# A two-layer hybrid transformer trunk on one core: where gathered rows and the router's input are transposed

## The reference, cut to what matters

```python
for l in range(DEPTH):                                  # DEPTH = 2
    h = _rmsnorm(x, mix_norm[l])
    ...                                                 # ya, yb, yc: the three mixers
    x = x + jnp.concatenate([ya, yb, yc], axis=-1) @ w_out[l]
    x = x + _expert_choice_ffn(_rmsnorm(x, ffn_norm[l]), router[l], w_gate[l], w_up[l], w_down[l])

def _expert_choice_ffn(x, router, w_gate, w_up, w_down):
    xf = x.reshape(T, D)
    aff = jax.nn.softmax((xf @ router).astype(jnp.float32), axis=-1)
    gate, idx = lax.top_k(aff.T, cap)                   # cap = 128 (sample) and 32 (prompt) per expert
    xs = xf[idx]
    hid = jax.nn.silu(jnp.einsum('ecd,edf->ecf', xs, w_gate)) * jnp.einsum('ecd,edf->ecf', xs, w_up)
    ye = jnp.einsum('ecf,efd->ecd', hid, w_down) * gate[..., None].astype(x.dtype)
    return jnp.zeros((T, D), x.dtype).at[idx.reshape(-1)].add(ye.reshape(-1, D)).reshape(B, S, D)
```

## Time and profile before

| | before |
|---|---|
| median of 3 runs (lowest, highest) | 2354.94 us (2353.14, 2355.67) |
| the profiled execution: its time, its span | 2355.69 us, 2354.1 us |
| PE busy | 2303.9 us (98%) |
| DVE busy | 995.4 us (42%) |
| ACT, POOL busy | 622.3 us (26%), 538.7 us (23%) |
| mean granted TensorE clock | 0.995 |
| DMA | 352.18 MB, mean 150 GB/s |

### The profile page before, as it was taken

The page is one execution under the profiler, slowest core; times in us unless marked ns, Lnnn a source line. Parts: engine busy times, 40 slices in busy tenths (PEclk is TensorE's granted clock), DMA queues, the critical chain, the costliest instruction groups (busy, mean ns, idle before and its releaser), DMA issues.

```text
span 2354.1 us, 33210 instructions
## 1 busy us (share of the span) xinstructions
PE 2303.9 (98%) x13054; PEld 1644.7 (70%) x13054; DVE 995.4 (42%) x1855; ACT 622.3 (26%) x1445; POOL 538.7 (23%) x550
## 2 busy tenths in 40 slices
PE   8999999999999999999999999999999999999998
PEld 6556587874556888877775665878655568887786
DVE  3654476586554111111136535756864631111111
ACT  3221333553342111111132312335533411111111
POOL 1003453243211111111110034632432111111111
PEclk9999999999999999999999999999999999999999
DMA  4011131221228988778430112312112389878883
GB/s 152 21 37 55 54 131 63 81 81 63 74 96 302 321 280 275 264 266 286 122 124 21 36 54 74 105 54 90 72 73 81 117 290 317 280 255 279 279 284 73
DMA packets 149364, 352.18 MB, mean 150 GB/s; under 512 B 9909, under 2 KB 38073, under 8 KB 149210
## 3 DMA queue, kind: packets, MB, share of 16 engines
q1 hardware_dynamic: 134234, 308.11, 36.6%
q0 software_dynamic: 14976, 41.95, 7.2%
HBM read 307.75 MB, written 42.28 MB: 149 GB/s over the span
## 4 chain that ended last, share of the span: by engine, by line
PE 93%; DVE 2%; DMA 1%; ACT 1%; issue 1%; POOL 0%; SPq 0%; DVEq 0%; ACTq 0%; POOLq 0%
PE ps L1813 88%; PE ps L2349 1%; PE ps L2098 1%; PE ps L2159 1%; PE ps L1832 1%; DVE TMP L1237 1%; DMA HT<-h_sample,idxs 0%; PE ps L1865 0%; DMA y_sample<-SCR,idxs 0%; PE ps L2110 0%; DVE TMP L1246 0%; PE ps L2339 0%; ACT SCR L1042 0%; DVE SCR L1237 0%; POOL SCR L759 0%
## 5 line engine op out<-in xcount | busy, mean ns | idle before, releaser
L1813 PE MATMUL ps<-MID,HT 128*128 128x512 f32 (+3 forms) x2560 | 693.2, 490 | 4.7 <-DMA MID<-w_in 3.8
L1813 PEld LDWEIGHTS ps<-HT,MID 128*128 128x128 f32 x4096 | 557.6, 191 | 16.1 <-issue 15.1
L1813 PE MATMUL ps<-HT,MID 128*128 128x160 f32 (+1 forms) x4096 | 565.6, 299 | 0.6 <-DVE HT L1237 0.4
L1813 PEld LDWEIGHTS ps<-MID,HT 128*128 128x128 f32 (+1 forms) x2560 | 292.6, 157 | 245.8 <-issue 207.2
L1813 PE MATMUL ps<-RING,HT 128*128 128x256 f32 (+2 forms) x1760 | 395.8, 392 | 1.7 <-DVE RING L1241 1.3
L1813 PEld LDWEIGHTS ps<-RING,HT 128*128 128x128 f32 (+1 forms) x1760 | 310.7, 189 | 83.5 <-issue 40.7
L1813 PE MATMUL ps<-HT,RING 128*128 128x512 f32 (+1 forms) x960 | 350.0, 522 | 0.0
L1246 DVE SCALAR_TENSOR_TENSOR HT<-HT,ps 128x160 f32<-128x160 f32 (+1 forms) x128 | 40.9, 319 | 683.1 <-ACT HT L1201 658.5
L1813 PEld LDWEIGHTS ps<-HT,RING 128*128 128x128 f32 x960 | 180.2, 190 | 157.8 <-issue 149.8
L849 POOL DMA_INDIRECT y_prompt<-SCR,idxp x32 | 50.5, 1578 | 618.4 <-ACT SCR L1211 617.8
L1201 ACT ACTIVATE HT<-ps 128x160 f32<-128x160 f32 (+1 forms) x128 | 38.6, 302 | 519.8 <-PE ps L1813 511.5
(11 more groups left out here) (264 smaller groups left out, 2159.3 us busy)
## 6 DMA issues: line engine op xcount, KB each, us to landing
MID<-w_gate SPq DMA_DIRECT2D x32, 2048.0 KB
MID<-w_up SPq DMA_DIRECT2D x32, 2048.0 KB
MID<-w_down SPq DMA_DIRECT2D x32, 2048.0 KB, 15.3
RING<-w_in SPq DMA_DIRECT2D x20, 1024.0 KB, 5.3
SCR<-cs_rows SPq DMA_DIRECT2D x20, 1024.0 KB, 5.1
MID<-w_out SPq DMA_DIRECT2D x8, 1024.0 KB, 6.6
y_sample<-RING SPq DMA_DIRECT2D x16, 512.0 KB, 2.7
h_sample<-HT SPq DMA_DIRECT2D x16, 512.0 KB, 2.6
```

Source lines behind the costliest of these rows:

```text
L1813: return pe.matmul(out, a, b, start=start, stop=stop)
```

## The change: what it does

In short:

- **Router input.** For chunks 0 to 6 of the attention stage PE's `turn_h2` and DVE's `keep_h2` go. DVE transposes `XO` itself: `turn_h2(c, a0, a1)` issues, for each group `a` of 32 rows, four transposes of 32 partitions by 256 elements (eight 32x32 blocks each), 16 for a chunk. Group 0 stands where `keep_h2(n-1, 0)` stood, group 1 behind `keep_y(n+1, 0)`, groups 2 and 3 behind `take_x(n)`. `logits` keeps its place on PE and its wait for `h2t_copied`, and from chunk 1 to 6 waits for `lg_shift` too. SP's reload of `XO` waits for DVE's transposes.
- **Gathered rows.** From expert 1 on the tokens, and from quad 1 on the prompt rows, are transposed by DVE straight from the gather buffer into `XT`: 8 transposes behind slice 1, 8 behind slice 2, for experts 4 and up 4 more for the prompt rows behind slice 3. Then two multiplications in place by the norm's weight (`weigh_tokens`). PE keeps the transposes of expert 0's tokens and of quad 0.
- **Last expert.** PE makes the prompt part first, then the two halves; ACT scales in that order; POOL scatters the sample rows in two halves of 512 columns, with row indices 2i and 2i+1 made by two small DVE operations (`idxh`).

The core of the diff (waits that are only renumbered are left out):

```diff
                         if c + 2 < NC:
                             sp.wait_ge(x_stored[c % 2], 16 * (c // 2 + 1))
-                            sp.wait_ge(h2t_made, 2 * c + 2)
+                            if c < LAST_SAMPLE:
+                                sp.wait_ge(h2t_copied, 2 * c + 2)
+                            else:
+                                sp.wait_ge(h2t_made, 2)
...
                     def gather(e):
                         if e >= 3:
-                            pool.wait_ge(g_turned, turn_at(e - 3, 1) + 1)
+                            if e == 3:
+                                pool.wait_ge(g_turned, 2)
+                            else:
+                                pool.wait_ge(xt_made, e - 3)
...
+                        if e == E - 1:
+                            pool.wait_ge(scattered_s, seen["halves"] + 16 * e)
+                            for hf in range(2):
+                                pool.wait_ge(down_scaled, 3 * e + 2 + hf)
+                                pool.indirect_dma_start(ys2, bass.IndirectOffsetOnAxis(ap=idxh[:, hf:hf + 1], axis=0),
+                                                        YO[e % 2][:, hf * 512:(hf + 1) * 512], None,
+                                                        compute_op=ALU.add, bounds_check=2 * SEQS[1] - 1).then_inc(scattered_s, 16)
+                            break
...
+                    def turn_h2(c, a0, a1):
+
+                        if a0 == 0 and c >= 1:
+                            dve.wait_ge(parts_made, c)
+                        for a in range(a0, a1):
+                            for b in range(4):
+                                turned = link(dve.transpose(H2T[32 * b:32 * b + 32, :, 32 * a:32 * a + 32],
+                                                            XO[c % 2][32 * a:32 * a + 32, :].rearrange("p (k b i) -> p k b i", b=4, i=32)[:, :, b, :]),
+                                              h2t_copied if b == 3 and a % 2 == 1 else dve_chain, wait=False)
...
                             attn_shift(n + 2, 0)
-                        keep_h2(n - 1, 0)
+                        turn_h2(n - 1, 0, 1)
                         keep_y(n + 1, 0)
+                        turn_h2(n - 1, 1, 2)
                         if n + 2 < NC:
                             attn_shift(n + 2, 1)
                         take_x(n)
-                        keep_h2(n - 1, 1)
+                        turn_h2(n - 1, 2, 4)
                         keep_y(n + 1, 1)
...
+                    for hf in range(2):
+                        ts(idxh[:, hf:hf + 1], idxs[:, E - 1:E], 2.0, float(hf), ALU.mult, ALU.add)
...
+                    def turn_rows(e, at, rows):
+
+                        for b in range(4):
+                            turned = link(dve.transpose(XT[e % 2][32 * b:32 * b + 32, :, at:at + 32],
+                                                        rows.rearrange("p (k b i) -> p k b i", b=4, i=32)[:, :, b, :]), wait=False)
+                        return turned
...
+                    def weigh_tokens(e, turned, cols):
+
+                        dve.wait_ge(dve_chain, turned)
+                        for j in range(2):
+                            v = XT[e % 2][:, 4 * j:4 * j + 4, 0:cols]
+                            tt(v, v, wide(pr("gffn")[:, 4 * j:4 * j + 4], cols), ALU.mult, xt_made if j == 1 else dve_chain)
...
-                            if f == KF - 3 and e + 1 < E:
-                                if (e + 1) % QUAD == 0:
-                                    for j in range(2):
-                                        copy_quad((e + 1) // QUAD, j)
-                                spread_quad(e + 1)
-                            if f == KF - 2 and e + 1 < E:
-                                copy_tokens(e + 1, 0)
+                            if e + 1 < E and 1 <= f <= 2:
+                                turned = turn_tokens(e + 1, 2 * f - 2, 2 * f)
...
-                        if e + 1 < E:
-                            copy_tokens(e + 1, 1)
+                        if e + 1 < QUAD:
+                            spread_quad(e + 1)
+                            weigh_tokens(e + 1, turned, CAPS)
+                        elif e + 1 < E:
+                            weigh_tokens(e + 1, turn_prompt(e + 1), TOK)
...
                         pe.wait_ge(h2t_copied, 2 * c + 2)
+                        if 1 <= c < LAST_SAMPLE:
+                            pe.wait_ge(lg_shift, c)
...
-                        turn_h2(n - 1, 0)
                         out_proj(n, 0, 5, 6)
...
                         out_proj(n, 0, 7, 8)
-                        turn_h2(n - 1, 1)
                         out_proj(n, 1, 0, 1)
...
                         if e >= 1:
-                            pe.wait_ge(g_copied, copied(turn_at(e, 1) + 1))
-                            pe.wait_ge(quad_spread, e + 2)
+                            pe.wait_ge(xt_made, e)
...
-                        else:
+                        elif e < E - 1:
                             down_half(0)
                             down_prompt()
+                            down_half(1)
+                        else:
+                            down_prompt()
+                            down_half(0)
                             down_half(1)
```

More of the change, by code:

```diff
@@ L162, in program @@
         idxp = sb("idxp", E, U32)
+        idxh = sb("idxh", 2, U32)
         idxus = sb("idxus", CAPS // 4 + CAPP, U32)
@@ L497, in counts @@
         def counts(layer):
-            return {"x": 16 * layer, "scatter": 16 * E * layer,
+            return {"x": 16 * layer, "scatter": 16 * E * layer, "halves": 16 * (E + 1) * layer,
                     "gather": [16 * layer * len(range(j, E, 3)) for j in range(3)],
@@ L567, in _ @@
                     else:
-                        sp.wait_ge(scattered_s, seen["scatter"])
+                        sp.wait_ge(scattered_s, seen["halves"])
                     for c in range(NP, NC):
@@ L676, in _ @@
                         pool.wait_ge(scattered_p, seen["scatter"])
-                        pool.wait_ge(scattered_s, seen["scatter"])
+                        pool.wait_ge(scattered_s, seen["halves"])
                     for r in RAW:
@@ L862, in _ @@
                         pool.wait_ge(scattered_p, seen["scatter"] + 16 * E)
-                        pool.wait_ge(scattered_s, seen["scatter"] + 16 * E)
+                        pool.wait_ge(scattered_s, seen["halves"] + 16 * (E + 1))
                     leave_layer(pool, layer)
@@ L1203, in _ @@
                             act.wait_ge(scattered_p, seen["scatter"] + 16 * (e - 1))
-                            act.wait_ge(scattered_s, seen["scatter"] + 16 * (e - 1))
+                            act.wait_ge(scattered_s, seen["halves"] + 16 * (e - 1))
                         def scale_half(hf):
@@ L1770, in spread_quad, with turn_tokens, turn_prompt @@
                         link(dve.tensor_copy(XT[e % 2][:, k0:k1, CAPS:TOK], XTP[:, k0:k1, CAPP * r:CAPP * (r + 1)]), quad_spread)
+                    def turn_rows(e, at, rows):
[3 more added lines that the diff above has]
+                        return turned
+                    def turn_tokens(e, a0, a1):
+                        if a0 == 0:
+                            dve.wait_ge(gathered[e % 3], seen["gather"][e % 3] + 16 * (e // 3 + 1))
+                        for a in range(a0, a1):
+                            turned = turn_rows(e, 32 * a, XG[e % 3][32 * a:32 * a + 32, :])
+                        return turned
+                    def turn_prompt(e):
+                        q, r = divmod(e, QUAD)
+                        dve.wait_ge(quad_gathered[q % 2], seen["quad"][q % 2] + 16 * (q // 2 + 1))
+                        return turn_rows(e, CAPS, XGP[q % 2][CAPP * r:CAPP * (r + 1), :])
+                    def weigh_tokens(e, turned, cols):
[3 more added lines that the diff above has]
+                            tt(v, v, wide(pr("gffn")[:, 4 * j:4 * j + 4], cols), ALU.mult, xt_made if j == 1 else dve_chain)
                     for e in range(E):
@@ L2406, in _ @@
                             last.then_inc(gu_made, 1)
-                            if f == KF - 3 and (e + 1) % QUAD == 0 and e + 1 < E:
-                                for j in range(2):
-                                    turn_quad((e + 1) // QUAD, j)
-                            if f == KF - 2 and 1 <= e < E - 1:
-                                turn_tokens(e + 1, 0)
                         if e == 0:
                             for j in range(2):
-                                turn_quad(0, j)
-                            turn_tokens(1, 0)
-                        elif e + 1 < E:
-                            turn_tokens(e + 1, 1)
+                                turn_quad(j)
                         pe.wait_ge([ed_loaded0, ed_loaded1][e % 2], 16 * (e // 2 + 1))
@@ L2436, in down_prompt @@
                             for f in range(KF):
+                                if e == E - 1:
```

(1 more changed line is left out.)

78 lines of the change are left out of this document (36 added, 42 removed).

## The result

The kernel after takes 2394.35 us (median of 4 runs, 2392.97 to 2395.47), the kernel before beside it 2355.09 (4 runs, 2353.14 to 2355.67): 1.0166 times as long, 95% interval 1.0154 to 1.0178. The forecast was 2375.5 in a range of 2336 to 2400, and slower. The profiled execution took 2395.1 us, its span is 2393.6, against 2354.1 before. So 39.5 us of span have to be found.

The account below looks back on a forecast made before the run. PE's instruction stream was taken as the bound. Experts and tail -36.6, chunk loop +45.1 and clock +12 gave net +20.5 on 2355.7 us, 2376.2, or 2375.5 as median; range 2336 to 2400.

Parts of the forecast that it names:

- What leaves PE: Removed PE transpose calls: 15.8 us per layer in the experts, about 1 in expert 0, 6.0 in the chunk loop.
- Rival E: Expert stage: PE's slots bring nothing because weight loads become the bound; 2407 us, chance 0.05.
- What a DVE transpose costs: Each 32x256 DVE transpose was put at a spacing of 0.45 us, a group of four at 1.8 us.
- C: DVE's transposes run as fast as its fast copy, spacing 0.20 us; 2321 us, chance 0.12.
- B: DVE's transposes overlap, spacing 0.335 us; 2348 us, chance 0.20.
- D: A DVE transpose costs 0.72 us, so HID is late in 14 experts per layer; 2513 us, chance 0.03.
- The wait on the router's product: Chunk loop: PE waits for DVE before logits in seven rounds, 28.6 us per layer, 22.6 net of saved slots.
- The clock: Chunk loop: the waits lower PE's clock, 1.7 us each; half of 14 falls taken, 12 us.
- the forecast of 24 to 25 us for a round: Sign in the chunk loop: rounds take 24 to 25 us in place of 21.4.
- Experts, DVE: Expert stage: DVE needs 4.3 us against PE's 4.35 per slice; HID of slice 3 keeps 0.9 us cover, cost 0.
- The last expert: Tail: scattering sample rows in two halves saves 1.5 us in each of two layers.
- forecast A: The main forecast: waits on logits outweigh the freed slots; own range 2363 to 2390 us, chance 0.60.

Follow-up runs that it names:

- experiment 2: Kernel before with only the gathered-row transposes moved to DVE; chunk loop, last expert's order and single scatter as before: 2321.85 us, ratio 0.9864.
- experiment 6: Kernel after with each DVE transpose of gathered rows issued as two of 32x128 on the same partitions: 2396.87 us in one run.
- Experiment 4: Kernel after with transpose groups 0 and 1 both ahead of keep_y(n+1, 0) on DVE: 2348.03 us, ratio 0.9978 to the kernel before.
- Experiment 5: Kernel after with six unread products of 384 columns on PE ahead of each router's product in the loop: 2364.97 us, ratio 1.0043 to before.

## Why the prediction was right, and where its size was off

**What leaves PE.** Right. Of PE's 480 transposes of these three kinds 80 are left, and the chain of the expert stage is one piece of PE (start, us, what), where the earlier trace rows shows it cut by calls of 0.44 us:

```profile
849.93 340.38 PE ps L1856 x2284
```

The down products of neighbouring experts start 26.31 us apart:

```profile
869.73 9.09 PE L1856 MATMUL ps<-MID,HT 128*128 128x512 f32 x48
896.04 9.09 PE L1856 MATMUL ps<-MID,HT 128*128 128x512 f32 x48
```

I had said 26.3. The two expert stages lost 34.0 us; 2 x (15.8 + 1) is 33.6, and experiment 2 gives 33.1. Rival E is refuted. One small thing was missing in the sum: before expert 0's first products PE now waits 0.51 us a layer for DVE's copy of the transposed rows, which it did not before.

**What a DVE transpose costs.** The group of the experts' transposes (count | busy, mean ns | idle before), after:

```profile
L1798 DVE STREAM_TRANSPOSE HT<-HT 32x256 f32<-32x256 f32 x576 | 251.0, 436 | 18.4
L1643 DVE STREAM_TRANSPOSE HT<-RING 32x256 f32<-32x256 f32 x224 | 97.6, 436 | 7.2
```

0.436 us against my 0.425 of the earlier trace rows, and four take 1.83, so a spacing of 0.46 to 0.47 against 0.45. C (0.20), B (0.335) and D (0.72) fall. The chain in expert 0 shows them one by one:

```profile
778.00 0.43 DVE HT L1798
778.46 0.43 DVE HT L1798
```

By that spacing the Trainium skill's rule ("VectorE: DVE Perf Modes", "Two Vector instructions with no wait between them") agrees with the trace, and experiment 6 shows both sides of it: 0.24 us apart at 0.30 us long on the same partitions, held until the end on others. The duration of a neighbour of its size (0.425) gave the duration here; whether the output's partitions change decides if the overlap comes off it.

**The wait on the router's product.** Right: 58.2 us in 14 waits against 2 x 28.6 = 57.2. Four a layer were put at 4.3 and are 4.32, the others at 3.75 to 3.95 and are 3.79 to 4.01. Experiment 4 confirms the geometry behind it, one T less for one group moved.

**The clock.** This is the step that failed, in its size. I priced a fall at 1.7 us from one short case and let half of the 14 waits bring one: 12 us. Both halves of that were too low. It fell in each of the 14 rounds, not in half of them, and the falls were dearer than 1.7 us. The loops grew by 79.2 us; less 58.2 of waits and plus 12.0 of freed slots (28 calls of 0.43), 33.0 are left. Experiment 5 gives 29.4 to 31.6 by taking the fall away and nothing else. That is 2.1 to 2.4 us a round where I had 0.85 on average. With it the sum would have come to 2393 to 2397. The rows above say why: from 608 to 620 the grant was 0.71, 0.50 and 0.94, which by my own measure is (0.29 + 0.50 + 0.06) x 4 = 3.4 us, twice the case of the earlier trace rows; only what lay in the wait cost nothing. Ten of the 14 rounds are of this kind. The other four are like the earlier trace rows, as round 7:

```profile
712.00:716.00 4.00, 0.01 (x1) 0.01 (x2) 3.72 (x10) 2.17 (x9) 0.00 (x0) 0.94 0.00 0
716.00:720.00 4.00, 4.00 (x35) 2.77 (x36) 1.16 (x4) 0.27 (x1) 1.89 (x1) 0.64 0.37 131
```

(0.06 + 0.36) x 4 is 1.7. One case with short gaps before it could not tell that a wait of 4 us brings the longer kind.

The same error is in the forecast of 24 to 25 us for a round: the slots and the wait make 21.4 + 4.3 - 0.9 = 24.8, and the clock makes it 27.4.

**Experts, DVE.** Right in that no later expert waits. Slice 3 and what lies behind it are covered by the down product. In expert 14, DVE's second eight transposes, then the two operations of HID of slice 3:

```profile
1156.31 3.71 DVE L1798 STREAM_TRANSPOSE HT<-HT 32x256 f32<-32x256 f32 x8
1160.05 0.32 DVE L1260 SCALAR_TENSOR_TENSOR HT<-HT,ps 128x160 f32<-128x160 f32 x1
1160.40 0.32 DVE L1251 TENSOR_TENSOR HT<-HT,ps 128x160 f32<-128x160 f32 x1
```

The down product of that expert starts at 1159.19 and comes to slice 3 three slices of 0.86 us later, at 1161.77. HID is there at 1160.72, so 1.05 us of cover are left, where I had 0.9. Experiment 6 used them up. PE's waits on DVE's two-operand line that writes this memory (L1251, before L1237) are 2.4 us in the whole kernel against 1.4, and none of them is in the experts' one long piece.

**The last expert.** Mechanism right, size short: 3.1 us in layer 0 and 1.3 in layer 1, 4.4 against 3.0 (4.6 by experiment 2). POOL's issues at the end, after, answering to the earlier trace rows:

```profile
2384.31 1.55 POOL L862 DMA_INDIRECT y_sample<-SCR,idxh  x1 [2.30 <-ACT SCR L1219]
2387.68 1.55 POOL L862 DMA_INDIRECT y_sample<-SCR,idxh  x1 [1.82 <-ACT SCR L1219]
```

The issue of half the bytes takes 1.55 us, as the whole did (1.56): the saving is in what comes behind it, 4.4 us to the end in place of 5.6. Why layer 0 saved more than twice that is open. There the scatter took 8.29 us from issue to landing before and its second half 5.15 after, and the next layer's load of prompt rows, which started with it before (1173.99 and 1174.00), now starts 3.35 us ahead of it; no run separates the two.

**Sum of the steps** (forecast, measured): waits net of slots +45.1, +46.2; clock +12, +33.0; experts and tail -36.6, -38.4. The 21 us missing in the forecast are one term. The result also lies above forecast A's own range, 2363 to 2390, whose upper end priced a fall in every round at 1.7 us. That it lies inside 2336 to 2400 is owed to the margin above 2390, which no term of the sum gave; that much is luck.

## What to carry to other kernels

Moving work from a full engine to one that is nearly idle pays where the receiver has a cover of its own, as here under the down product, and costs the whole delay where the result sits between two steps of the full engine: ask when the other engine delivers, not how busy it is. A wait of some microseconds on TensorE has two prices, its length and the low clock behind it; here waits of 3.8 to 4.3 us brought a fall each time, and PE's work behind them paid about half the wait's length again. Filling such a wait with useless work gave that half back. If the delay stays, place the consumer later, but recount what its old neighbours now run into.

## What the runs showed of the hardware that was not expected

- One idle stretch of 3.8 to 4.3 us behind a busy one brought the low level of TensorE's clock all 14 times, about 2.1 to 2.4 us of loss each. Waits of 1.9 to 2.7 us brought it in 5 of 14 rounds, all five behind waits of about 2.46 us and none behind the two of 2.67, with the runs of that kernel spread over 9 us where the others spread over 1.4 to 5.4.
- A DVE operation on 128x384 with both operands and the output in SBUF took 0.56 us in the mean of its 12 places after, and 1.32 in the mean of the same 12 before. One case before, round n = 3, POOL and DVE:

```profile
597.80 2.75 POOL L759 TENSOR_TENSOR SCR<-SCR,small 128x1536 f32<-128x1536 f32 x1 [7.71 <-DVE small L1563]
...
598.97 1.99 DVE L1237 TENSOR_TENSOR TMP<-MID 128x384 f32<-128x384 f32 x1
```

It runs beside POOL's scaling of the probabilities, and ends 0.41 us behind it (600.96 and 600.55). So it does in experiment 5, where it starts at 608.54, takes 1.43 and ends 0.40 behind POOL's. Where the delayed DVE starts behind POOL's operation, as at 615.62 in the kernel after, it takes 0.56; where it starts 0.11 us ahead (before, 1710.89), it takes 0.56 too and POOL's takes 3.05 in place of 2.75. DVE's neighbours that read PSUM keep their length beside the same POOL operation (0.42 us at 598.51). All of this fits that of the two the one that starts later waits for the other. No experiment isolated it, so that is a reading, not shown.
